# Expert stage of a mixture-of-experts step: tokens gathered in quarter rows and turned on VectorE instead of TensorE, padded slots left out of gather and store

## The reference, cut to what matters

```python
def block(args):                      # 128 slots of one expert
    tok, g, e = args
    xb = t_pad[tok]                   # rows of the normed tokens
    hb = silu(xb @ wg[e]) * (xb @ wu[e])
    return (hb @ wd[e]) * g[:, None]
...
out = zeros((T + 1, D)).at[slot_tok].add(yb.reshape(P, D))
```

## Time and profile before

| what | value |
|---|---|
| median of 3 runs (least, most) | 2407.86 us (2405.62, 2410.89) |
| span of the profiled execution | 2407.8 us |
| its own time | not listed apart from the span; the median is 0.06 us above the span |
| PE busy | 2067.2 us, 86% of the span |
| DVE, ACT, POOL busy | 662.9, 395.2, 361.5 us |
| expert stage, first to last gate/up lap begin | 1490.25 to 2284.83 us |

### The profile page before, as it was taken

One profiled execution on the slowest core, in us unless ns is written; L12 is line 12 of the kernel. 1 busy time (PEld: TensorE's weight loads), 2 busy tenths in 40 slices (PEclk: granted clock), 3 DMA queues, 4 the chain that ended last, 5 costly groups with the idle time before them and its releaser, 6 DMA issues. The chain is left out here.

```text
span 2407.8 us, 24712 instructions
## 1 busy us (share of the span) xinstructions
PE 2067.2 (86%) x7963; PEld 1176.2 (49%) x7964; DVE 662.9 (28%) x1074; ACT 395.2 (16%) x721; POOL 361.5 (15%) x496
## 2 busy tenths in 40 slices
PE   7999973788871466999998886999999999999965
PEld 2255542788870353555554453444444444444422
DVE  0300046344535773111111571111111111111126
ACT  1000034111112211000000211211212112121210
POOL 0000000332320320000000132111111111111134
PEclk9999975899995678999999988999999999999988
DMA  9411110000000013111113004999988999799856
GB/s 367 183 53 61 61 43 0 3 1 1 1 3 1 0 46 146 66 54 65 59 61 132 27 9 163 348 363 369 361 309 301 361 367 365 263 350 342 281 212 248
DMA packets 210855, 388.16 MB, mean 161 GB/s; under 512 B 12633, under 2 KB 146233, under 8 KB 210286
## 3 DMA queue, kind: packets, MB, share of 16 engines
q1 hardware_dynamic: 183234, 291.76, 34.8%
q0 software_dynamic: 27568, 95.68, 11.0%
HBM read 342.41 MB, written 45.00 MB: 161 GB/s over the span
## 5 line engine op out<-in xcount | busy, mean ns | idle before, releaser
L1831 PE MATMUL ps_gu_b<-we_gu,xgT 128*128 x1120 | 491.3, 597 | 6.9 <-DMA we_gu<-we_up 3.5
L1831 PEld LDWEIGHTS ps_gu_b<-we_gu,xgT 128*128 128x128 f32 x1120 | 210.6, 190 | 285.0 <-issue 284.9
L1265 PE MATMUL ps_logit<-hT_back,w_merge_tiles 128*128 128x512 f32 (+1 forms) x1024 | 284.4, 436 | 19.3 <-DMA w_merge_tiles<-w_merge 19.3
L1847 PE MATMUL ps_y_b<-we_dn,hsT_b 128*128 x560 | 258.5, 594 | 2.2 <-issue 2.2
L1265 PEld LDWEIGHTS ps_logit<-hT_back,w_merge_tiles 128*128 128x128 f32 x1024 | 158.1, 192 | 142.9 <-issue 123.5
L296 PE MATMUL ps_turn_and_in<-hT,w_tiles 128*128 128x512 f32 x704 | 190.6, 434 | 0.0
L1917 DVE TENSOR_TENSOR hs_b<-sg_b,ps_gu_b 128x256 f32<-128x256 f32 x70 | 29.5, 421 | 526.5 <-ACT sg_b L1885 526.5
L296 PEld LDWEIGHTS ps_turn_and_in<-hT,w_tiles 128*128 128x128 f32 x704 | 106.3, 191 | 85.0 <-issue 85.0
L1847 PEld LDWEIGHTS ps_y_b<-we_dn,hsT_b 128*128 128x128 f32 x560 | 98.7, 191 | 86.5 <-issue 86.5
L1796 POOL DMA_DIRECT2D y_dram<-y_b x70 | 40.5, 578 | 664.9 <-ACT y_b L1893 431.9
L1297 DVE TENSOR_TENSOR merge_part<-merge_gate,ps_proj 128x640 f32<-128x640 f32 x32 | 26.3, 821 | 304.3 <-ACT merge_gate L1284 304.3
(11 more groups left out here) (403 smaller groups left out, 2267.0 us busy)
## 6 DMA issues: line engine op xcount, KB each, us to landing
we_gu<-we_gate SPq DMA_DIRECT2D x64, 1024.0 KB, 9.0
we_gu<-we_up SPq DMA_DIRECT2D x64, 1024.0 KB, 11.5
we_dn<-we_down SPq DMA_DIRECT2D x128, 512.0 KB, 8.5
y_dram<-y_b POOLq DMA_DIRECT2D x70, 512.0 KB, 7.4
wmod<-w_mod SPq DMA_DIRECT2D x12, 2048.0 KB, 13.4
w_merge_tiles<-w_merge SPq DMA_DIRECT2D x32, 640.0 KB, 3.8
w_tiles<-w_mix SPq DMA_DIRECT2D x22, 512.0 KB, 3.2
proj<-x_sample SPq DMA_DIRECT2D x2, 2048.0 KB, 18.8
```

Of the source, the lines that this page charges most:

```text
L1265: pe.matmul(ps_l[:, b, lo:hi], w[:, b, k * P:(k + 1) * P], hT[:, k, lo:hi], start=(k == 0), stop=(k == KD - 1))
L1831: mm = pe.matmul(ps_gu[:, b, :], xT[:, b, k, :], w_gu[:, bass.ds(half[b], 1), k, :].rearrange("p a n -> p (a n)"), start=(k == 0), stop=(k ...
L1847: mm = pe.matmul(ps_y[:, c * 512:(c + 1) * 512], hsT[:, b, k * P:(k + 1) * P], w_dn[:, bass.ds(half[b], 1), k, c * 512:(c + 1) * 512].rear ...
```

## The change

1. The list is filled with T = 640 (a token that does not exist) instead of 0. Slots with that number are out of the bounds that the indirect DMAs now carry, and are passed over by them.
2. A gather is four indirect DMAs over quarter rows (`quarters`, 1 KB each): DMA q fetches the slots 32q to 32q+31, and partition 32a+s gets quarter a of slot 32q+s. One DVE instruction then transposes all 32x32 squares of `xg` into `xT`. PE's turns, `ps_x` and ACT's `copy_x` are gone. `xg` is cleared once at the start.
3. `y` is stored with an indirect DMA to the rows of the valid slots; the padded ones get a row number above the bounds (`NO_ROW`). The waits between stores are gone.
4. The indices for both come from one preparation at the stage's start: four broadcast copies of the list, two more small DVE operations, four more PE matmuls, one wide DVE operation.
5. PE's lap is re-ordered: `turn_hs(0)` sits before the last two matmuls of `gate_up(1)`; ACT's second sigmoid stands behind `copy_hs(0)`.

The core of the diff (file's line numbers shift by 7 to 29 from here on):

```diff
-                pool.memset(zero_u[:], 0).then_inc(zeroed, 1)
+                pool.memset(none_u[:], T).then_inc(zeroed, 1)
...
+                ch.link(dve.tensor_copy(m.place[:, 0:2], rc[:, N_EXP:N_EXP + 2]))
...
+                ch.link(dve.tensor_copy(m.place[:, 2:3], c(B_ROW)))
...
+                pool.memset(xg[:], 0.0).then_inc(pool_done, 1)
...
-                    pool.tensor_copy(idx[:, b, :], idx_all[:, bass.ds(2 * i + b, 1)]).then_inc(pool_done, 1)
+                    pool.tensor_copy(idx_x[:, b, :], all_x[:, bass.ds(2 * i + b, 1), :].rearrange("p a q -> p (a q)")
+                                     ).then_inc(pool_done, 1)
...
-                    pool.indirect_dma_start(xg[:, b, :], None, m.h2_dram,
-                                            bass.IndirectOffsetOnAxis(ap=idx[:, b, :], axis=0)
-                                            ).then_inc(gathered[b], 16)
+                    for q in range(4):
+                        pool.indirect_dma_start(xg[:, b, q, :], None, quarters,
+                                                bass.IndirectOffsetOnAxis(ap=idx_x[:, b, q:q + 1], axis=0),
+                                                bounds_check=4 * T - 1, oob_is_err=False).then_inc(gathered[b], 16)
+
+                def store(b, i, done):
+                    for c in range(2):
+                        pool.wait_ge(y_half_ok[c][b], i + 1)
+                    pool.wait_ge(pool_done, done)
+                    pool.tensor_copy(idx_y[:, b, :], all_y[:, bass.ds(2 * i + b, 1), :].rearrange("p a q -> p (a q)")
+                                     ).then_inc(pool_done, 1)
+                    pool.wait_ge(pool_done, done + 1)
+                    pool.tensor_add(tick[:], m.zero[:], m.zero[:]).then_inc(pool_done, 1)
+                    pool.indirect_dma_start(m.y_dram, bass.IndirectOffsetOnAxis(ap=idx_y[:, b, 0:1], axis=0),
+                                            y[:, b, :], None, bounds_check=T * TOP_K - 1, oob_is_err=False
+                                            ).then_inc(y_store[b], 16)
...
-                        pool.wait_ge(turned[b], i + 1)
-                        gather(b, i + 1)
+                        pool.wait_ge(xT_ok[b], i + 1)
+                        gather(b, i + 1, 8 * i + 6 + 2 * b)
                     for b in range(2):
-                        at = entry(pool, 2 * i + b, B_ROW, 0, T * TOP_K + T - P)
-
-                        pool.wait_ge(y_store[1 - b], 16 * (i + b))
-                        for c in range(2):
-                            pool.wait_ge(y_half_ok[c][b], i + 1)
-                        pool.dma_start(m.y_dram[bass.ds(at, P), :], y[:, b, :]).then_inc(y_store[b], 16)
+                        store(b, i, 8 * i + 10 + 2 * b)
...
+                for q in range(4):
+                    pe.matmul(ps_list[:, 0, q * P:(q + 1) * P], list_4[:, q].rearrange("p a s -> p (a s)"), ident,
+                              start=True, stop=True)
+                pe.transpose(ps_list[:, 1, 0:P], row_f[:], ident).then_inc(list_turn, 1)
...
+                    ready(0)
+                    gate_up(0, range(KD)).then_inc(gu_mm, 1)
+                    ready(1)
+                    gate_up(1, range(KD - 2))
                     turn_hs(0)
-                    turn(0, i + 1)
+                    gate_up(1, range(KD - 2, KD)).then_inc(gu_mm, 1)
                     down(0, 0)
                     turn_hs(1)
                     down(0, 1)
-                    turn(1, i + 1)
                     down(1, 0)
                     down(1, 1)
...
+                dve.tensor_scalar(all_x[:].rearrange("p r q -> p q r"),
+                                  ps_list[:, 0, :].rearrange("p (q r) -> p q r", q=4),
+                                  4.0, m.place[:, 1:2], ALU.mult, ALU.add)
...
+                def turn(b, i):
+                    dve.wait_ge(gathered[b], 64 * i + 64)
+                    dve.transpose(xT[:, b].rearrange("p k q s -> p q k s"),
+                                  xg[:, b].rearrange("p q (f k) -> p q k f", k=KD)).then_inc(xT_ok[b], 1)
...
                         dve.tensor_copy(y[:, b, 0:512], ps_y[:, 0:512]).then_inc(y_half_ok[0][b], 1)
+                        turn(b, i + 1)
```

More of the change, by code:

```diff
@@ L1700, in experts @@
         w_dn = a.sb("we_dn", [P, 2, 2, D])
[L1701 to L1704, removed]
+        idx_x, idx_y = a.sb("idx_x", [P, 2, 4], U32), a.sb("idx_y", [P, 2, 1], U32)
+        list_u, list_f, row_f = a.sb("list_u", [P, P], U32), a.sb("list_f", [P, P]), a.sb("row_f", [P, P])
+        list_4 = a.sb("list_4", [P, 4, 4, 32])
+        all_x, all_y = a.sb("all_x", [P, P, 4], U32), a.sb("all_y", [P, P, 1], U32)
+        xg = a.sb("xg", [P, 2, 4, QW])
+        xT = a.sb("xgT", [P, 2, KD, 4, 32])
         sg, hs, hsT = a.sb("sg_b", [P, 2, FF]), a.sb("hs_b", [P, 2, FF]), a.sb("hsT_b", [P, 2, FF])
         y = a.sb("y_b", [P, 2, D])
-        ps_x = a.ps("ps_x", [P, 2, D])
+        ps_list = a.ps("ps_list", [P, 2, 512])
         ps_gu = a.ps("ps_gu_b", [P, 2, 2 * FF])
         ps_y = a.ps("ps_y_b", [P, D])
[L1710 to L1713, removed]
+        (gu_in, dn_in, gathered, xT_ok, sig_ok, mul_ok, hs_ok, hs_turned, hsT_ok, y_store) = (
+            a.ring(f"b_{n}", 2) for n in (
+                "gu_in", "dn_in", "gathered", "xT_ok", "sig_ok", "mul_ok", "hs_ok", "hs_turned", "hsT_ok", "y_store"))
         gu_mm, y_mm = a.sems("b_gu_mm", "b_y_mm")
@@ L1808, in _, with gate_up, ready @@
                 pe.wait_ge(list_turn, 1)
-                pe.transpose(ps_gu[:, 0, 0:P], list_f[:], ident).then_inc(list_turn, 1)
-                def turn(b, i):
-                    pe.wait_ge(gathered[b], 16 * i + 16)
-                    for k in range(KD):
-                        mm = pe.transpose(ps_x[:, b, k * P:(k + 1) * P], xg[:, b, k::KD], ident)
-                    mm.then_inc(turned[b], 1)
-                for b in range(2):
-                    turn(b, 0)
+                for q in range(4):
+                    pe.matmul(ps_list[:, 0, q * P:(q + 1) * P], list_4[:, q].rearrange("p a s -> p (a s)"), ident,
+                              start=True, stop=True)
+                pe.transpose(ps_list[:, 1, 0:P], row_f[:], ident).then_inc(list_turn, 1)
                 def lap(i):
                     half, loads = [0, 0], [0, 0]
-                    for b in range(2):
+                    def gate_up(b, ks):
+                        for k in ks:
+                            mm = pe.matmul(ps_gu[:, b, :], xT[:, b, k].rearrange("p q s -> p (q s)"),
+                                           w_gu[:, bass.ds(half[b], 1), k, :].rearrange("p a n -> p (a n)"),
+                                           start=(k == 0), stop=(k == KD - 1))
+                        return mm
+                    def ready(b):
                         blk = 2 * i + b
@@ L1829, in lap @@
                         pe.wait_ge(hsT_ok[b], i)
-                        for k in range(KD):
-                            mm = pe.matmul(ps_gu[:, b, :], xT[:, b, k, :],
-                                           w_gu[:, bass.ds(half[b], 1), k, :].rearrange("p a n -> p (a n)"),
-                                           start=(k == 0), stop=(k == KD - 1))
-                        mm.then_inc(gu_mm, 1)
                     def turn_hs(b):
@@ L1872, in _, with gate @@
                 n = laps(act)
-                def copy_x(b, i):
-                    act.wait_ge(turned[b], i + 1)
-                    act.activation(xT[:, b].rearrange("p k t -> p (k t)"), ps_x[:, b, :], ACT.Copy
-                                   ).then_inc(xT_ok[b], 1)
-                for b in range(2):
-                    copy_x(b, 0)
                 def lap(i):
-                    for b in range(2):
+                    def gate(b):
                         act.wait_ge(gu_mm, 2 * i + b + 1)
@@ L2078, in trunk_kernel @@
             m.list_row = whole.sb("list_row", [P, 1], U32)
+            m.place = whole.sb("place", [P, 3])
             m.laps = whole.sb("laps", [P, 2], I32)
```

49 lines of the change are left out of this document (31 added, 18 removed).

## The result

| | before | after |
|---|---|---|
| median of the runs, us | 2408.74 (2405.62 to 2410.89) | 2369.58 (2367.03 to 2371.70) |
| ratio to before | | 0.9837, 95% interval 0.9823 to 0.9851 |
| span of the profiled execution, us | 2407.8 | 2365.2 |
| plain lap, us | 22.99 | 22.10 |

The kernel is 39 us faster by the medians, 42.6 by the two profiled executions. The time lies inside the range, 0.7% above the forecast. The lap does not: 21.2 to 21.4 was forecast, and a lap above 22 was named as what would make the prediction wrong.

A forecast was written before the change was run, and what follows sets the result against it. PE's own work was taken to bound the 22.99 us lap, DMA close behind. From 2407.8: -62.0 (turns), +4 (DMA), +1 (start), +1 (end), +0.2 (routing) gave 2352.0 us, range 2335 to 2380.

The forecast's parts named there:

- a lap above 22: Sign on PE's lap: 21.2 to 21.4 us was forecast, above 22 would make the prediction wrong.
- PE's turns: PE's lap: removing both turns saves 1.77 us in each of 35 laps, -62.0 us, leaving 21.22 us.
- The new order: PE's re-ordered lap: both `turn_hs` covered, taken as 0; up to 7 us if a semaphore hop is paid.
- The turn on DVE: DVE's transposition: 1.3 us taken, 1.22 to 2.04 possible, hidden and free up to 4.4 us.
- POOL: POOL's issuing of gathers and stores: 14.6 of 21.2 us a lap, gathers landing 6.0 us later, hidden, no cost.
- the fourth and fifth case: POOL becomes the bound, kernel slower at 2485 us, chance 0.05; the gain lost to late gathers, chance 0.03.
- DMA: DMA engines: a lap with loads needs 20.2 of 21.2 us; +4 us for uneven laps, ends 0 and 12.
- the 13 us of uneven laps: Laps before averaged 0.38 us above the plain lap, 13 us in all; left in, their loss the lower end.
- Passed-over rows not free: Rival on DMA: padded slots still take engine time, a lap needs 22.6 us, 2393 us in all; chance 0.15.
- The argument against it: Against passed-over rows costing DMA time: rows are separate pieces already, and a piece not made needs no engine.
- Stores not relieved: Rival on stores: engines tied to partitions, a store takes full time, 2355 to 2380, put at 2366 us; chance 0.15.
- Start, end, rest: Stage start: later first gather, +1 us; stage end: later last store, +1 us; routing: two DVE copies, +0.2 us.

The follow-up runs named there:

- e1: Changed kernel with a separate PSUM buffer for each block's down product, so the lap's last wait names an older copy: 2337.26 us, ratio 0.9705.
- e4: Changed kernel with PE's and ACT's order of the kernel before, turns still gone: 2398.74 us, ratio 0.9956.
- e2: Changed kernel with each transposition on DVE made twice, one behind the other: 2372.50 us, ratio 0.9851.
- e5: Kernel before, with one of the eight transpositions in each turn of a lap, order kept, outputs not the reference's: 2408.74 us, ratio 1.0000.
- e6: Kernel before, with only the changed kernel's order of PE's and ACT's work, turns kept: 2410.45 us, ratio 1.0007.
- e11: Changed kernel, its one PSUM buffer kept, with padded slots gathering the last token's row and padded rows of y stored: 2376.53 us, ratio 0.9861.
- e7: e1 with padded slots gathering the last token's row instead of being passed over: 2353.23 us, ratio 0.9771.
- e9: e7 with padded slots fetching 320 different rows in turn instead of one row: 2349.42 us, ratio 0.9748.
- e8: e1 with padded rows of y also stored, to rows of their own that nothing reads: 2339.19 us, ratio 0.9719.
- e3: Changed kernel with one more table read by PE's sequencer at each lap's begin (four loads for three): 2397.94 us, ratio 0.9955.

## Why the prediction was right and where it failed

The sign, the range and the hidden parts were right. The sum came out 13.2 us too low against the profiled execution, because a miss of 30 us was half made good by gains that were not forecast. That the sum came so near is luck; the step that carried it failed.

- **PE's turns, -62.0: the step that failed.** It says "The lap that is left is 21.22 us". The lap is 22.10, and the turns brought 34 x 0.89 = 30.3 us in the laps and 1.8 in the last, which has no next gate/up to wait for: 32.0. The step took PE's idle-free timeline as proof that "PE's own work is the lap". It was one of two ways round, 22.83 us long, and the other, with ACT's copy and the table reads behind a semaphore wait, set the lap at 22.99. One turn, ahead of `down(0,0)`, stood in both ways, and its 0.88 us are the gain that came; the other, behind `down(0,1)`, stood in the first way only. It left a trace in a row that I had before me: the last lap's gate/up waited 1.01 us for "issue", and I read it as unevenness. Beside the one wait for weights that it names, 3.5 us, PE also had 3.2 us of "issue" before gate/up. e1 gives 32 us back, and its lap of 21.06 is the forecast's 21.22 without the 0.16 that the old lap waited.
- **The new order, 0 (to 7).** It costs nothing, as taken: `turn_hs(1)` at 1642.45 follows `down(0,0)` without a gap. But it was priced as a cost alone. It is a condition of the gain: without it (e4) the change is worth 11 us and not 39.
- **The turn on DVE, 1.3 between 1.22 and 2.04.** Measured 2.01, at the strided end; hidden, as both ends were said to be, and e2 shows that even twice of it is.
- **POOL.** The indirect DMAs take 1.01 us (median) and follow each other every 1.3; the gathers land after 4.6 us, sooner than the 6.0 taken. PE waits for turned rows once, at the start. POOL isn't the bound and the gathers are not late: the fourth and fifth case fall.
- **DMA, +4 on top of the 13 us of uneven laps.** The first 34 laps last 756.45 us (1491.98 to 2248.43), 5.1 above 34 plain ones, where the kernel before had 12.9: -7.9 and not +4. The forecast put the 12.9 to the queues, but 5.3 of them stand in one lap, the 29th (28.32 us). There POOL's store went out later than elsewhere (10.03 us idle before it, 7.33 in the earlier trace rows), the gather stands behind it in POOL's order, and PE waited for its rows:

```profile
2147.20 0.57 POOL L1796 DMA_DIRECT2D y_dram<-y_b  x1 [10.03 <-issue]
...
2148.54 1.04 POOL L1779 DMA_INDIRECT xg<-h_dram,idx_b  x1 [0.31 <-POOL tick L1778]
...
2156.14 1.97 PE L1814 MATMUL ps_x<-const,xg 128*128 128x128 f32 x8 [2.72 <-DMA xg<-h_dram,idx_b]
```

  That lap takes 28.3 to 30.8 us in the three kernels with the old gathers and stores (before, e5, e6) and is a plain lap in all with the new, also in e11, which has the bytes back. So these 5.3 us are not the bytes'; which part of the change takes them away, and what made the store late, no run isolates. For the rest, a lap of 22.10 leaves the queues nearly 2 us, by the forecast's own need of 20.2, and e11's uneven laps, with the bytes back, lose 4.0 us more than the change's. The bytes fell as forecast: gathers and stores of before were 142 transfers of 0.52 MB, 74.4; POOL's queue carries 32.4 MB less than the 95.68 of before, so 56% are left.
- **Passed-over rows not free** falls: e7 and e9 fetch them and pay 12 to 16 us, and the packets' share rises with them. The argument against it was not right as it stood: a passed-over piece is still a packet, only a short one. **Stores not relieved** has no price here: e8 stores every row whole and its lap stays 21.06, where that rival needs 21.3 or more. Whether the engines are tied to partitions, as the Trainium skill has it (DMA: Bandwidth & Descriptors, section The descriptor swizzle) for a transfer that writes 128 partitions, no run shows for a store, which reads them; a full store costs nothing either way. The rival's ends, 2355 and 2380, also count the forecast's +4 in one and not in the other.
- **Start, end, rest.** The first gate/up comes 1.7 us later (+1 forecast); e6, which leaves the start as it was, has it 3.2 us later, so this is within the scatter of the stages ahead. The last store ends 2.9 us behind the start of ACT's copy, 1.9 before: +1.0, as forecast:

```profile
1491.98 1.22 PE L1836 MATMUL ps_gu_b<-we_gu,xgT 128*128 x1 [14.40 <-DVE xgT L1936]
...
2269.79 0.60 ACT L1903 ACTIVATE y_b<-ps_y_b 128x512 f32<-128x512 f32 x1 [2.75 <-PE ps_y_b L1862]
...
2271.69 1.01 POOL L1801 DMA_INDIRECT y_dram<-y_b,idx_y  x1 [0.54 <-issue]
```

What follows the last store, to the end of the program, is 5.4 us shorter (92.5 for 97.9), which nothing forecast; 1.3 of it lie ahead of combine's first gather, the rest I did not trace to a cause. The account: 30.0 (lap) - 11.9 (unevenness) + 0.7 (start) - 5.4 (combine) - 0.2 (routing, not seen) = 13.2 us above the forecast.

## What to carry to other kernels

An engine without a gap shows that its work fills the lap, not that nothing else is as long, and its rows can even hide a short wait. Before pricing the removal of work, walk the loop's other ways round, through the last wait in the engine's instruction stream and all register reads, branches and waits that stand behind it. A wait that the matmuls never feel still holds the sequencer, and what it holds comes due when the work that covered it goes. Here the cure was one more PSUM buffer, so that the lap's last wait names something long done.

## What the runs showed of the hardware that was not expected

- A table entry read into a register of PE's sequencer costs 0.75 us with its register instructions (0.30 the load itself); one more of them a lap made each plain lap 0.67 us longer (e3).
- The sequencer's time is in no busy figure; the gap that it leaves is named "issue", or after any transfer that happens to end near it (e3, e5).
- DVE's transposition of 128 x 1024 fp32 with a strided read takes 2.01 us, about as much as two strided reads of 512 (1.02 each).
- A row that the bounds check passes over is still a packet: 16 bytes and 10.5 ns in a gather, where 4 KB take 172 ns (e1).
- The 16 DMA engines moved 379 GB/s over 100 us in this mix (e8); and nearly the same bytes cost 16 us as gathers and nothing measurable as stores (e7, e8).
